# The pooling branch as fp32 matmuls over tokens, in place of GpSimd's running sums

## The chip, the cores and the metric

The kernel runs on one core of a Trainium2 chip. A core has five engines that run side by side, each from a queue of its own in order: TensorE (PE, with PEld for its weight loads), VectorE (DVE), ScalarE (ACT), GpSimd (POOL) and SyncE (SP, which issues most DMAs). They wait for each other by semaphores. The metric is the device time of one execution in microseconds (us).

## The reference, cut to what matters

Three blocks in a row over 256 tokens of width 1024, in fp32: one block of a first kind, then two layers of a second kind. Each layer of the second kind is a feed-forward, a mixer, a cross attention and a feed-forward. The mixer adds three gated branches; the change is in the pooling branch, which takes 1024 of the mixer's input columns in four groups of 256:

```python
POOL_WINDOWS = (2, 4, 8, 16)
def pool_branch(u, w_grp, scale, w_o):
    uf = u.astype(jnp.float32).reshape(B, S, POOL_GROUPS, POOL_GD)
    cz = jnp.pad(jnp.cumsum(uf, axis=1), ((0, 0), (1, 0), (0, 0), (0, 0)))
    for g, w in enumerate(POOL_WINDOWS):
        c = cz[:, :, g]
        prev = jnp.pad(c, ((0, 0), (w - 1, 0), (0, 0)))[:, :S]
        cnt = jnp.minimum(t + 1, w).astype(jnp.float32)[None, :, None]
        outs.append((c[:, 1:] - prev) / cnt)
    pooled = (jnp.stack(outs, axis=2) - uf).astype(u.dtype)
    y = jnp.einsum('bsgc,gcd->bsgd', pooled, w_grp).reshape(B, S, POOL_D) * scale
    return y @ w_o
```

So group g is the mean over the last 2, 4, 8 or 16 tokens (fewer at the start), less the token itself, and then a 256x256 product per group (`pool_w`), a scale and a 1024x1024 product (`pool_o`).

## The kernel before

Activations lie with features on the 128 partitions and the 256 tokens along the free axis. Every large product is made of *units*: 4 slices of 128 rows of the weight by 256 columns. SP loads a unit's weights (`raw_weights`, six buffers), ScalarE rounds them to a high half (L1096), DVE subtracts to get the low half (L1413; four buffers of each), three units ahead of PE. PE then runs 24 matmuls (L842, or L845 where the activations are the stationary operand and the result lies token by token, the "T form"): high by high, low by high, high by low. A `pool_w` unit has half of that, 12. One or more units that fill one of the two accumulator slots of `gemm_ps` are a *pair*; its first unit waits until the pair two before it has been copied out.

`plan` writes one list of steps, and each engine walks that list and issues its part of each step. In the mixer the list is the branch inputs, the two-map attention of eight heads spread between units, and 40 pieces of a depthwise convolution of 31 taps, each piece three taps on two features, six DVE instructions (L1854). A head is: scores on PE (L969 and L970, eight fp32 matmuls, waiting for the previous head's exponentials), row maxima on DVE (L1612), exponentials on ScalarE (L1219), normalisation on DVE, transposes on PE (the turn, L987), a copy on ScalarE (L1229), the product with the values (L1007, L1008), and the copy of the output on DVE (L1664). Every second head a norm follows (L1017 on PE, Ln and Exp with a table load each on ScalarE, L1673 on DVE).

The part that the change touches, `queries_pool`: pool group 3, group 2, query block 1, group 1, group 0, query blocks 2 and 3, two units each. DVE copies a group out of the accumulator with the token's scale (L1860), GpSimd adds shifted copies of it in `squares` (L1985, one to four doublings), multiplies by 1/count (L1990) and subtracts the input (L1993). After query block 3 ScalarE rounds the pooled tiles to `gh` (L1171, eight of them) and DVE makes `gl` (L1550, eight), and `pool_w` follows. GpSimd issues the loads of the attention bias and of the counts at the mixer's start; for the rest it only splits the feed-forward's hidden tiles.

Of the kernel before, what the change touches and what calls it, by code (L numbers as in the profile page):

```python
# [37 lines left out]
POOL_PAD = 15  # L38
# [48 lines left out]
def plan(stop=None):  # L87
# [468 lines left out]
def build(nc, a, out, scratch, marks, final, stop=None):  # L556
# [24 lines left out]
    def overlay(**shapes):  # L581

        with ExitStack() as c:
# [17 lines left out]
                  pu=[P, NF, POOL_PAD + T], tmp2=[P, NF, T], gt2=[P, 2, 2, T], bt2=[P, 2, T],  # L601
                  cnt=[P, 4, T])
# [7 lines left out]

    wide = POOL_PAD + T
    WIN = [SQ[:].rearrange("p f t -> p (f t)")[:, i * 2 * wide:(i + 1) * 2 * wide].rearrange("p (a t) -> p a t", a=2)
           for i in range(2)]
    RT8 = sb("adapt_gain", [P, NF])
    MGS = {"b1": SQ[:], "m": o_m["pu"][:, :, POOL_PAD:]}
# [47 lines left out]
    def xbuf(buf, gen):  # L663
        if buf == "G":
            return (o_b1["gh"], o_b1["gl"]) if gen in ("oa", "ob", "oc") else (o_m["gh2"], o_m["gl2"])
        if buf == "HID":
# [5 lines left out]
           "xk": o_c["xk"], "xv": o_c["xv"], "memf": o_c["memf"], "pooled": o_m["tmp2"], "TMP": o_m["tmp2"],  # L672
# [45 lines left out]
    def ready_of(k):  # L718
# [4 lines left out]
                "xq": ("o", "cross" + gen[1], f // 2), "pooled": ("pooled", gen[:2], f // 2),  # L723
# [22 lines left out]
    def _(sp):  # L746
# [29 lines left out]
        for u in raws:  # L776
# [21 lines left out]
            dst = RAWB[:, r % RAW, 0:u["nkt"], :]  # L798
# [7 lines left out]
            else:  # L806
                sp.dma_start(dst[:, :, 0:u["cols"]], w[:, :, u["col"]:u["col"] + u["cols"]]).then_inc(sems[sem], 16)
# [7 lines left out]
    def _(pe):  # L815
# [6 lines left out]
        def pe_unit(u):  # L822
# [10 lines left out]
            for c in range(tiles):  # L833
                for kt in range(u["nkt"]):
# [3 lines left out]
                    for n, (w, x) in enumerate(((WH, xh), (WH, xl), (WL, xh))):  # L838
# [5 lines left out]
                        else:  # L844
                            mm = pe.matmul(ps[:, c, 0:u["cols"]], x[:, f, c * P:(c + 1) * P],  # L845
                                           w[:, m, kt, 0:u["cols"]], start=start, stop=stop_)
            mm.then_inc(sems["gemm_done"], 1)
            up("gemm_done", ("unit", u["n"]))

# [226 lines left out]
        parts = dict(unit=pe_unit, params=pe_params, turn_x=pe_turn_x, mod=pe_mod, mod_col=pe_mod_col, bias=pe_bias, stat=pe_stat, ystat=pe_ystat,  # L1076
# [9 lines left out]
    def _(act):  # L1086
        state = dict(rq=None)
        def hi(m):
# [6 lines left out]
            s = (slice(None), m % SPLIT, slice(0, u["nkt"]), slice(0, u["cols"]))  # L1095
            act.copy(WH[s], RAWB[:, u["raw"] % RAW, 0:u["nkt"], 0:u["cols"]]).then_inc(sems["weights_rounded"], 1)  # L1096
# [278 lines left out]

        def act_evac_pool_w(k):
# [683 lines left out]
```

## Time and profile before

| | |
|---|---|
| median of 3 runs | 2508.78 us (2506.63 to 2510.61) |
| the profiled execution | 2511.45 us |
| its span, first to last instruction | 2509.6 us |
| PE busy | 2341.3 us (93%) |
| DVE busy | 1716.7 us (68%) |
| ACT busy | 1201.1 us (48%) |
| POOL busy | 136.8 us (5%) |

Busy time is a share of the whole span; what a wait costs is read in the stretch where it stands. The two mixers run from about 820 us and 1760 us; the pooling inputs stand at 919 to 1001 us and 1858 to 1942 us.

### The profile page before, as it was taken

The numbers are of one execution on the slowest core, as the hardware profiler recorded it, in microseconds if no ns is written. First come the engines' busy times: TensorE is split into PE (matmuls) and PEld (weight loads), VectorE is DVE, ScalarE is ACT, GpSimd is POOL, SyncE is SP. The second block draws the span as 40 slices with busy tenths as digits, with TensorE's granted clock in tenths as the row PEclk, the third lists the DMA queues.
The fourth block names the chain that finished last, engine by engine and source line by source line (L and its number), as shares of the span: only waits on it lengthen the run. The fifth ranks groups of instructions, "written<-read, shape, count | busy, mean of one in ns | idle before, by whom it ended". The sixth has DMA issues, their size and how long they took to land.

```text
span 2509.6 us, 43811 instructions
## 1 busy us (share of the span) xinstructions
PE 2341.3 (93%) x18041; PEld 2243.3 (89%) x18041; DVE 1716.7 (68%) x2665; ACT 1201.1 (48%) x1811; POOL 136.8 (5%) x114
## 2 busy tenths in 40 slices
PE   6998898999999988999998999999988999998997
PEld 5977898999999987889898998999987889898997
DVE  6656886886664897887555654664896877555663
ACT  2565445764444433555535444444433455535443
POOL 1000000110110012000000110110012000000110
PEclk9998999999999998999999999999997999999999
DMA  8534574667656552345444654656452336443652
GB/s 243 171 110 141 162 250 150 190 184 226 185 170 203 154 162 76 126 128 185 143 144 126 186 185 143 185 174 204 152 160 76 118 123 191 135 145 123 189 179 85
DMA packets 402038, 400.38 MB, mean 160 GB/s; under 512 B 18006, under 2 KB 399304, under 8 KB 401841
## 3 DMA queue, kind: packets, MB, share of 16 engines
q1 hardware_dynamic: 399457, 389.27, 50.3%
q0 software_dynamic: 2384, 8.32, 1.1%
q8 instruction: 144, 2.36, 0.4%
q14 instruction: 53, 0.43, 0.1%
HBM read 396.45 MB, written 1.09 MB: 158 GB/s over the span
## 4 chain that ended last, share of the span: by engine, by line
PE 71%; DVE 19%; ACT 5%; issue 4%; DMA 1%; ACTq 0%; POOL 0%; DVEq 0%; POOLq 0%
PE gemm_ps L842 59%; DVE weights_lo L1413 5%; DVE y L1854 4%; PE misc_ps L970 2%; PE misc_ps L969 2%; PE gemm_ps L845 2%; PE misc_ps L913 2%; DVE mod_partial L1510 1%; PE misc_ps L922 1%; ACT weights_hi L1096 1%; DVE y L1566 1%; ACT e L1219 1%; DVE x_res L1568 1%; ACT h_hi L1171 1%; PE misc_ps L1002 1%
## 5 line engine op out<-in xcount | busy, mean ns | idle before, releaser
L1413 DVE TENSOR_TENSOR weights_lo<-raw_weights,weights_hi 128x1024 fp32r<-128x1024 f32 x704 | 837.6, 1200 | 470.5 <-ACT weights_hi L1096 468.6
L842 PE MATMUL gemm_ps<-h_hi,weights_hi 128*128 128x256 f32 x3664 | 1054.3, 288 | 53.6 <-DVE h_lo L1547 37.3
L1096 ACT CAST weights_hi<-raw_weights 128x1024 fp32r<-128x1024 f32 x704 | 718.8, 1033 | 682.4 <-PE gemm_ps L842 623.6
L842 PE MATMUL gemm_ps<-h_lo,weights_hi 128*128 128x256 f32 x3664 | 1038.3, 283 | 0.0
L842 PE MATMUL gemm_ps<-h_hi,weights_lo 128*128 128x256 f32 x3664 | 1035.9, 283 | 0.0
L842 PEld LDWEIGHTS gemm_ps<-h_hi,weights_hi 128*128 128x128 f32 x3664 | 703.6, 192 | 64.9 <-issue 48.7
L842 PEld LDWEIGHTS gemm_ps<-h_lo,weights_hi 128*128 128x128 f32 x3664 | 703.4, 192 | 3.3 <-issue 2.2
L842 PEld LDWEIGHTS gemm_ps<-h_hi,weights_lo 128*128 128x128 f32 x3664 | 701.2, 191 | 0.0
L842 PE MATMUL gemm_ps<-hidh,weights_hi 128*128 128x256 f32 x880 | 247.8, 282 | 1.5 <-DVE weights_lo L1413 1.5
L842 PE MATMUL gemm_ps<-hidl,weights_hi 128*128 128x256 f32 x880 | 245.9, 279 | 0.0
L842 PE MATMUL gemm_ps<-hidh,weights_lo 128*128 128x256 f32 x880 | 245.7, 279 | 0.0
L1854 DVE SCALAR_TENSOR_TENSOR y<-zp,param_cols,y 128x256 f32<-128x256 f32 x480 | 213.0, 514 | 0.0
L842 PE MATMUL gemm_ps<-gh,weights_hi 128*128 128x256 f32 x544 | 163.3, 300 | 18.2 <-DVE gl L1550 14.7
L842 PEld LDWEIGHTS gemm_ps<-hidh,weights_hi 128*128 128x128 f32 x880 | 165.3, 188 | 1.9 <-DVE weights_lo L1413 1.7
L842 PEld LDWEIGHTS gemm_ps<-hidl,weights_hi 128*128 128x128 f32 x880 | 165.0, 187 | 0.2
L842 PEld LDWEIGHTS gemm_ps<-hidh,weights_lo 128*128 128x128 f32 x880 | 165.0, 188 | 0.0
L842 PE MATMUL gemm_ps<-gl,weights_hi 128*128 128x256 f32 x544 | 156.9, 288 | 0.0
L842 PE MATMUL gemm_ps<-gh,weights_lo 128*128 128x256 f32 x544 | 156.5, 288 | 0.0
L1970 POOL TENSOR_TENSOR hidl<-hf,hidh 128x512 fp32r<-128x512 f32 x55 | 73.6, 1337 | 1260.0 <-ACT hidh L1344 1260.0
L842 PEld LDWEIGHTS gemm_ps<-gh,weights_hi 128*128 128x128 f32 x544 | 107.7, 198 | 21.6 <-issue 19.2
L842 PEld LDWEIGHTS gemm_ps<-gl,weights_hi 128*128 128x128 f32 x544 | 107.8, 198 | 1.3 <-issue 1.0
L842 PEld LDWEIGHTS gemm_ps<-gh,weights_lo 128*128 128x128 f32 x544 | 107.4, 197 | 0.0
(284 smaller groups left out, 2580.6 us busy)
## 6 DMA issues: line engine op xcount, KB each, us to landing
raw_weights<-in_ffn_w_dram SPq DMA_DIRECT2D x256, 512.0 KB, 3.7
raw_weights<-in_w_in_dram SPq DMA_DIRECT2D x200, 512.0 KB, 3.6
raw_weights<-in_w_mod_dram SPq DMA_DIRECT2D x48, 512.0 KB, 5.2
raw_weights<-in_w_up_dram SPq DMA_DIRECT2D x44, 512.0 KB, 4.5
raw_weights<-in_xattn_kv_dram SPq DMA_DIRECT2D x32, 512.0 KB, 4.2
raw_weights<-in_w_out_dram SPq DMA_DIRECT2D x24, 512.0 KB, 4.5
raw_weights<-in_w_down_dram SPq DMA_DIRECT2D x20, 512.0 KB, 4.9
raw_weights<-in_w_branch_dram SPq DMA_DIRECT2D x16, 512.0 KB, 4.5
```

Of the source, the lines that this page charges most:

```text
L842: mm = pe.matmul(ps[:, c, 0:T], w[:, m, kt, c * P:(c + 1) * P], x[:, f, :], start=start, stop=stop_)
L845: mm = pe.matmul(ps[:, c, 0:u["cols"]], x[:, f, c * P:(c + 1) * P], w[:, m, kt, 0:u["cols"]], start=start, stop=stop_)
L913: mm = pe.matmul(STAT[:, 0:T], ONES[:], squares[:, f, :], start=f == 0, stop=f == NF - 1)
L922: mm = pe.matmul(STAT[:, 0:T], ONES[:], SQ[:, f, :], start=f == 0, stop=f == NF - 1)
L969: pe.matmul(ps, c["q"][m][:, qt * P:(qt + 1) * P], c["k"][m][:, 0:nk], start=True, stop=False)
L970: mm = pe.matmul(ps, FLIP[:], c["hank"][:, c["head"][m], T - nk:T], start=False, stop=True)
L1002: mm = pe.matmul(PV[:, f * T:(f + 1) * T], c["v"][f][kb], PT[:, kb * T:(kb + 1) * T], start=kb == 0, stop=kb == 1)
L1096: act.copy(WH[s], RAWB[:, u["raw"] % RAW, 0:u["nkt"], 0:u["cols"]]).then_inc(sems["weights_rounded"], 1)
L1171: act.activation(h[:, k["ft0"] + f, :], src, ACT.Copy, scale=col(c[0], c[1] + f) if c else scale).then_inc(sems["act_split"], 1)
L1413: dve.tensor_tensor(WL[s], RAWB[:, u["raw"] % RAW, 0:u["nkt"], 0:u["cols"]], WH[s], ALU.subtract).then_inc(sems["weights_rest"], 1)
L1854: dve.scalar_tensor_tensor(out=Y[:, f, :], in0=o_m["zp"][:, f, j:j + T], scalar=col(f"dw{l}", 8 * j + f), in1=Y[:, f, :], op0=ALU.mult, op ...
L1970: pool.tensor_tensor(l_[:, s, :], src, h[:, s, :], ALU.subtract).then_inc(sems["hidden_rest"], 1)
```

## The change

The constant 256x256 matrix of a group holds 1/count where the token is within the window, less the identity. Pooling is then a product over tokens, for which the input must lie with tokens on the partitions. So the pool inputs are computed in the T form, in two pairs of 512 columns (groups 2 and 3, then 0 and 1), each of four units of 2 slices by 512 columns, 12 matmuls each. DVE copies such a pair out with two instructions. A new step `window` per group runs four fp32 matmuls on PE: the matrix is lower triangular in tokens, so the second half of the tokens needs only 128 result columns. Its result takes an accumulator slot. ScalarE rounds it from there to `gh` and DVE subtracts to `gl`; the eight splits are gone, and so are GpSimd's sums. The load of the counts becomes one of the matrices, 128x1536 numbers instead of 128x1024.

```diff
         def queries_pool():
-            for name, j in (("pool", 3), ("pool", 2), ("q", 1), ("pool", 1), ("pool", 0), ("q", 2), ("q", 3)):
-                if name == "q":
-                    z2(l, "q", j, "evac_scaled", dst="q", ft=2 * j, by=HD ** -0.5)
-                else:
-                    z2(l, "pool", j, "evac_pool", ft=2 * j)
-                    add("window", g=j, l=l)
-            for g in (3, 2, 1, 0):
-                for f in (2 * g, 2 * g + 1):
-                    add("split", buf="G", gen=key + "p", src="pooled", f=f, ft0=0, after=readers.get("G"), v=0)
+            after = readers.get("G")
+            def inputs(j):
+                z2(l, "pool", j, "evac_v2", form="T", cols=2 * COLS, dst="pt", c0=j * COLS)
...
+            def window(g):
+                p = dict(id=len(pairs), l=l, g=g, gen=key + "p", after=after)
+                pairs.append(p)
+                add("window", **p)
+                add("evac_window", **p)
+            inputs(2)
+            query(1)
+            window(3)
+            inputs(0)
+            window(2)
+            query(2)
+            window(1)
+            query(3)
+            window(0)
...
+        def pe_window(k):
+            ps, u, g = GP[:, k["id"] % 2, :, :], BUF["pt"], k["g"]
+            pe.wait_ge(*done(("evac", k["id"] - 2)))
+            pe.wait_ge(*done(("tm", "pt", k["l"], g * COLS)))
+            pe.wait_ge(sems["windows_in"], at("win", k["l"]))
+            for i in range(2):
+                f = 2 * g + i
+                pe.matmul(ps[:, i, 0:T], u[:, 0, f * P:(f + 1) * P], o_m["win"][:, g, 0:T], start=True, stop=False)
+                mm = pe.matmul(ps[:, i, P:T], u[:, 1, f * P:(f + 1) * P], o_m["win"][:, g, T:T + P], start=False, stop=True)
...
+        def act_window(k):
+            f = 2 * k["g"]
+            act.wait_ge(sems["gemm_done"], at("pooled", k["l"], k["g"]))
...
+            act.copy(o_m["gh2"][:, f:f + 2, :], slot(k["id"])).then_inc(sems["act_split"], 1)
...
+        def vec_window(k):
+            f = 2 * k["g"]
+            dve.wait_ge(sems["act_split"], at("split_hi", "G", k["gen"], f))
+            dve.tensor_tensor(o_m["gl2"][:, f:f + 2, :], slot(k["id"]), o_m["gh2"][:, f:f + 2, :], ALU.subtract).then_inc(sems["vec_split"], 1)
...
+            mark(("evac", k["id"]), "vec_split")
```

Where it moves instructions. On PE in layer 0, behind query block 1 and the value product of head 0, before (L842: a unit; `vec_conv` is the copy-out of pool group 2, long before):

```order
L1007 MATMUL misc_ps<-pt,v 128x256 [waits act_attn]
L1008 MATMUL misc_ps<-pt,v 128x128
L842 MATMUL gemm_ps<-h_hi,weights_hi 128x256 [waits vec_split,vec_conv,weights_rest]
L842 MATMUL gemm_ps<-h_lo,weights_hi 128x256
L842 MATMUL gemm_ps<-h_hi,weights_lo 128x256
```

The same place of the change (L876, L877: the window; `pu` holds the inputs token by token; L863: a wide unit; its `vec_drain` is now the copy-out of query block 1):

```order
L1038 MATMUL misc_ps<-pt,v 128x256 [waits act_attn]
L1039 MATMUL misc_ps<-pt,v 128x128
L876 MATMUL gemm_ps<-win,pu 128x256 [waits windows_in,vec_drain]
L877 MATMUL gemm_ps<-win,pu 128x128
L876 MATMUL gemm_ps<-win,pu 128x256
L877 MATMUL gemm_ps<-win,pu 128x128
L863 MATMUL gemm_ps<-weights_hi,h_hi 128x512 [waits vec_split,vec_drain,weights_rest]
```

The four matmuls of group 3 have moved in as a pair of their own, and the pair behind them waits for another copy-out than before.

On DVE, from the softmax of head 1 to the convolution piece behind, before:

```order
L1648 SCALAR_TENSOR_TENSOR e<-e,rden 128x256
L1664 COPY q<-misc_ps 128x256
L1594 SCALAR_TENSOR_TENSOR q<-gemm_ps,rstd_x 128x512
L1413 TENSOR_TENSOR weights_lo<-raw_weights,weights_hi 128x1024 x2
L1854 SCALAR_TENSOR_TENSOR y<-zp,param_cols,y 128x256 x6
L1860 TENSOR_TENSOR pu<-gemm_ps,rstd_x 128x2x256
```

and of the change:

```order
L1687 SCALAR_TENSOR_TENSOR e<-e,rden 128x256
L1703 COPY q<-misc_ps 128x256
L1632 SCALAR_TENSOR_TENSOR q<-gemm_ps,rstd_x 128x512
L1898 TENSOR_TENSOR gl<-gemm_ps,gh 128x512
L1451 TENSOR_TENSOR weights_lo<-raw_weights,weights_hi 128x1024 x2
L1891 SCALAR_TENSOR_TENSOR y<-zp,param_cols,y 128x256 x6
```

The copy-out of query block 1 (L1594, now L1632) stands where it stood, behind the softmax; the subtraction of window 3 follows it, and the copy-out of a pool group behind the convolution piece is gone.

On PE in front of `pool_w`, the change has window 0 between the value product of head 2 and the first `pool_w` matmul:

```order
L1039 MATMUL misc_ps<-pt,v 128x128
L876 MATMUL gemm_ps<-win,pu 128x256 [waits windows_in,vec_drain,vec_split]
L877 MATMUL gemm_ps<-win,pu 128x128
L876 MATMUL gemm_ps<-win,pu 128x256
L877 MATMUL gemm_ps<-win,pu 128x128
L860 MATMUL gemm_ps<-gh,weights_hi 128x256 [waits vec_split,vec_drain,weights_rest]
```

Before, `pool_w` stood right behind the value product. Its `vec_drain` is the copy-out of query block 3, its `vec_split` the pooled low half.

## Rows read from the trace of the kernel before

**Rows 1.** The page's chain of work that ended last, by engine.

```profile
PE 71%; DVE 19%; ACT 5%; issue 4%; DMA 1%; ACTq 0%; POOL 0%; DVEq 0%; POOLq 0%
```

**Rows 2.** PE's waits, 905 to 1060 us: total, times, longest in us.

```profile
PE gemm_ps L842 <- DVE gl L1550: 7.4, 1, 7.4
PE misc_ps L969 <- ACT e L1219: 6.8, 2, 6.1
```

**Rows 3.** The same view, 1845 to 2000 us.

```profile
PE misc_ps L969 <- ACT e L1219: 7.6, 2, 6.7
PE gemm_ps L842 <- DVE gl L1550: 7.3, 1, 7.3
```

**Rows 4.** DVE's timeline, layer 0: start us, duration us, instruction.

```profile
927.75 0.69 DVE L1860 TENSOR_TENSOR pu<-gemm_ps,rstd_x 128x512 f32<-128x512 f32 x1
...
929.49 7.90 DVE L1854 SCALAR_TENSOR_TENSOR y<-zp,param_cols,y 128x256 f32<-128x256 f32 x6
937.31 1.01 DVE L1612 TENSOR_REDUCE neg_max<-misc_ps 128x2 f32<-128x256 f32 x2
...
942.85 2.46 DVE L1854 SCALAR_TENSOR_TENSOR y<-zp,param_cols,y 128x256 f32<-128x256 f32 x6
```

**Rows 5.** GpSimd's timeline, the sums of group 3.

```profile
928.53 2.00 POOL L1985 TENSOR_TENSOR squares<-pu 128x540 f32<-128x540 f32 x1 [118.54 <-DVE pu L1860]
...
935.87 1.24 POOL L1993 TENSOR_TENSOR tmp<-tmp,pu 128x512 f32<-128x512 f32 x1
```

**Rows 6.** PE's timeline: scores (L969), turns (L987), the norm's sum (L1017), `pool_w` (gh).

```profile
924.33 0.48 PE L969 MATMUL misc_ps<-k,q 64*128 64x128 f32 x2
...
940.13 0.79 PE L969 MATMUL misc_ps<-k,q 64*128 64x128 f32 x2 [6.11 <-ACT e L1219]
...
951.59 0.49 PE L987 MATMUL misc_ps<-ident,e 128*128 128x128 f32 x3
...
962.66 0.46 PE L969 MATMUL misc_ps<-k,q 64*128 64x128 f32 x2 [1.45 <-DVE q L1594]
...
982.22 0.49 PE L969 MATMUL misc_ps<-k,q 64*128 64x128 f32 x2
...
989.13 0.49 PE L987 MATMUL misc_ps<-ident,e 128*128 128x128 f32 x3
989.46 1.02 PE L1017 MATMUL misc_ps<-small_squares,ones 128*128 128x512 f32 x2
...
1001.28 0.55 PE L842 MATMUL gemm_ps<-gh,weights_hi 128*128 128x256 f32 x1 [7.42 <-DVE gl L1550]
...
1863.42 0.48 PE L969 MATMUL misc_ps<-k,q 64*128 64x128 f32 x2
...
1941.97 0.55 PE L842 MATMUL gemm_ps<-gh,weights_hi 128*128 128x256 f32 x1 [7.32 <-DVE gl L1550]
```

**Rows 7.** The chain that ended last, in order of time: start us, us, what.

```profile
952.08 2.83 PE gemm_ps L842 x24
954.91 0.43 PE misc_ps L1007 x2
955.34 0.22 PE misc_ps L1008 x2
...
961.92 0.61 DVE q L1594
```

**Rows 8.** Stretches: length, busy us of PE, PEld, DVE, ACT, POOL, PEclk, DMA share, GB/s.

```profile
940.10:951.60 11.50, 11.47 (x41) 8.44 (x42) 6.86 (x15) 1.86 (x2) 5.24 (x5) 0.56 0.30 93
1001.20:1005.90 4.70, 4.62 (x24) 4.52 (x24) 4.70 (x13) 1.86 (x4) 0.00 (x0) 0.61 0.14 24
1020.40:1030.50 10.10, 10.04 (x62) 8.03 (x63) 9.98 (x22) 6.38 (x11) 0.00 (x0) 1.00 0.34 104
1941.90:1947.30 5.40, 5.33 (x25) 5.23 (x25) 5.40 (x15) 1.94 (x4) 0.00 (x0) 0.53 0.27 72
1961.70:1971.80 10.10, 10.07 (x41) 7.78 (x42) 10.02 (x22) 3.81 (x6) 0.00 (x0) 0.66 0.33 105
```

More of the change, by code:

```diff
@@ L37 @@
 FFN_K = 3
-POOL_PAD = 15
 LAYERS = 2
@@ L609, in build @@
     o_b1["bt1"] = o_b1["rg"][:, 0]
-    wide = POOL_PAD + T
-    WIN = [SQ[:].rearrange("p f t -> p (f t)")[:, i * 2 * wide:(i + 1) * 2 * wide].rearrange("p (a t) -> p a t", a=2)
-           for i in range(2)]
     RT8 = sb("adapt_gain", [P, NF])
-    MGS = {"b1": SQ[:], "m": o_m["pu"][:, :, POOL_PAD:]}
+    MGS = {"b1": SQ[:], "m": o_m["pu"][:]}
     last_x = max([k["v"] for kind, k in steps if kind == "residual"], default=0)
@@ L683, in slot, with unit_of @@
         return GP[:, pid % 2, :, 0:T]
+    def unit_of(buf, i, u):
+        if u["cols"] <= COLS:
+            return buf[:, i, 0:u["nkt"], 0:u["cols"]]
+        wide = buf[:, i].rearrange("p k n -> p (k n)").rearrange("p (k n) -> p k n", n=u["cols"])
+        return wide[:, 0:u["nkt"], :]
     def att(cfg, i):
@@ L1074, in pe_finish @@
             up("pe_setup", ("out_ps",))
-        parts = dict(unit=pe_unit, params=pe_params, turn_x=pe_turn_x, mod=pe_mod, mod_col=pe_mod_col, bias=pe_bias, stat=pe_stat, ystat=pe_ystat,
+        parts = dict(unit=pe_unit, window=pe_window, params=pe_params, turn_x=pe_turn_x, mod=pe_mod, mod_col=pe_mod_col, bias=pe_bias, stat=pe_stat, ystat=pe_ystat,
                      rstd_cols=pe_rstd_cols, qk_norm=pe_qk_norm, scores=pe_scores, turn=pe_turn, pv=pe_pv,
@@ L1374, in act_cln_out @@
             up("act_conv", ("cln_tanh", l, p))
+        def act_window(k):
+            f = 2 * k["g"]
+            act.wait_ge(sems["gemm_done"], at("pooled", k["l"], k["g"]))
+            if k["after"] is not None:
+                act.wait_ge(sems["gemm_done"], at("unit", k["after"]))
+            act.copy(o_m["gh2"][:, f:f + 2, :], slot(k["id"])).then_inc(sems["act_split"], 1)
+            up("act_split", ("split_hi", "G", k["gen"], f))
         def act_evac_pool_w(k):
@@ L1600, in vec_v2 @@
             for t in range(TT):
-                dve.tensor_scalar(BUF[k["dst"]][:, t, k["c0"]:k["c0"] + COLS], slot(k["id"])[:, t, :], RT[:, t:t + 1], None, ALU.mult).then_inc(sems["vec_drain"], 1)
+                dve.tensor_scalar(BUF[k["dst"]][:, t, k["c0"]:k["c0"] + k["cols"]], GP[:, k["id"] % 2, t, 0:k["cols"]], RT[:, t:t + 1], None, ALU.mult).then_inc(sems["vec_drain"], 1)
                 up("vec_drain", ("evac", k["id"]))
             mark(("tm", k["dst"], k["l"]), "vec_drain")
-            mark(("tm", k["dst"], k["l"], k["c0"]), "vec_drain")
+            for c in range(k["c0"], k["c0"] + k["cols"], COLS):
+                mark(("tm", k["dst"], k["l"], c), "vec_drain")
         def vec_softmax(k):
@@ L1856, in vec_conv31 @@
             mark(("conv", l), "vec_conv")
[L1858 to L1862 removed]
+        def vec_window(k):
+            f = 2 * k["g"]
+            dve.wait_ge(sems["act_split"], at("split_hi", "G", k["gen"], f))
+            dve.tensor_tensor(o_m["gl2"][:, f:f + 2, :], slot(k["id"]), o_m["gh2"][:, f:f + 2, :], ALU.subtract).then_inc(sems["vec_split"], 1)
+            up("vec_split", ("split", "G", k["gen"], f))
+            mark(("split", "G", k["gen"], f + 1), "vec_split")
+            mark(("evac", k["id"]), "vec_split")
         def vec_pool_w(k):
@@ L1949, in pool_hankel @@
             if k["which"] == 2:
-                pool.dma_start(o_m["cnt"][:], bass.AP(tensor=a["inv_count"].tensor, offset=0, ap=[[0, P], [1, 4 * T]])).then_inc(sems["count_in"], 16)
-                up("count_in", ("cnt", k["l"]), by=16)
+                pool.dma_start(o_m["win"][:], a["windows"]).then_inc(sems["windows_in"], 16)
+                up("windows_in", ("win", k["l"]), by=16)
         def pool_blocks(k):
@@ L2033, in shape_constants @@
     t = np.arange(T)
-    inv = np.stack([(1.0 / np.minimum(t + 1, w)).astype(np.float32) for w in (2, 4, 8, 16)])
+    windows = []
+    for w in (2, 4, 8, 16):
+        behind = t[None, :] - t[:, None]
+        share = (1.0 / np.minimum(t + 1, w)).astype(np.float32)
+        m = np.where((behind >= 0) & (behind < w), share[None, :], np.float32(0.0)) - np.eye(T, dtype=np.float32)
+        windows.append(np.concatenate([m[:P], m[P:, P:]], axis=1))
+    windows = np.ascontiguousarray(np.stack(windows, axis=1).astype(np.float32))
     return {"ident": np.eye(P, dtype=np.float32), "flip": np.ascontiguousarray(np.eye(P, dtype=np.float32)[::-1]),
-            "headsum": heads, "onehot": np.ascontiguousarray(onehot), "inv_count": inv}
+            "headsum": heads, "onehot": np.ascontiguousarray(onehot), "windows": windows}
 def declare(nc, arrays):
```

70 lines of the change are left out of this document (23 added, 47 removed).

## The prediction

> **What bounds the kernel now.** The first view is the page's chain that ended last: 71% of it is TensorE (PE), 19% VectorE (DVE), and nothing to speak of is GpSimd (POOL) [rows 1]. So GpSimd's sums are worth nothing by themselves; they count where they hold up DVE, and through it PE. The next view is PE's waits inside the two mixers, where the change lies. Layer 0: 7.4 us once for the low half `gl` of the pooled input, and 6.8 us for ScalarE's exponentials `e`, of which 6.1 in one wait [rows 2]; layer 1: 7.3 and 7.6, of which 6.7 in one [rows 3]. The third view says why the exponentials are late. DVE's queue is in order: copy-out of pool group 3 at 927.75, a weight subtraction, six convolution taps, then the row maxima that ScalarE's exponentials wait for. Those six taps took 7.90 us; the same six took 2.46 us at 942.85 [rows 4]. In just that time GpSimd ran the sums of group 3, from 928.53 to 937.11 [rows 5]. So 5.44 us of the first wait are GpSimd's doing.
>
> The Trainium skill says that GpSimd shares its SBUF interfaces with VectorE and contends with DVE instructions that have two SBUF inputs ("GPSIMD Engine Reference", section 8, Key points). The taps read two, and [rows 4, 5] agree with it in direction; by that page alone the change could only be a gain.
>
> **The yardstick.** I measure from the first score matmul of head 0 (call it A: 924.33 and 1863.42) to the first `pool_w` matmul (1001.28 and 1941.97) [rows 6]. That is 76.95 us in layer 0 and 78.55 us in layer 1. I build the same stretch for the changed kernel out of pieces of this trace.
>
> **Prices.** A unit of 24 matmuls of 256 columns is 2.83 us, 0.118 us each [rows 7]. A wide unit is 12 of 512 columns, which no row shows. Upper bound: twice 0.118, so 2.83 us again. Lower bound: the fp32 rows take 0.22 us for 128 columns and 0.43 for 256 [rows 7], time in proportion to columns with the weight load hidden; at half of 0.43 for 512 columns of this type, 12 x 0.215 = 2.6 us. I take 2.7. A window group is two matmuls of 256 and two of 128 columns in fp32; the attention value product is one of each, with the same operand shapes, at 0.43 + 0.22 = 0.65 us [rows 7], so 1.3 us a group. If they went like the scores, whose eight matmuls (four of 256 columns, four of 128) are 6.91 - 2.83, some 3.9 to 4.1 us (982.22 to 989.13, less a unit) [rows 6, 7], four would be 2.0 us; the shapes speak for 1.3. The four groups are 5.2 us a layer of new PE work. A DVE read of 512 columns from PSUM is 0.61 us in the chain [rows 7].
>
> **What the change puts in the way.** The accumulator has two slots, and a pair (a set of units that fills one slot) waits until the pair two before it is copied out. Before, the pair between was always two units, 5.65 us of cover. Now each window is a pair of its own, of only 1.3 us. So the unit behind window 3 waits for the copy-out of query block 1, the unit behind window 2 for that of the pool inputs 0 and 1, and `pool_w` behind window 0 for that of query block 3. All three copy-outs stand on DVE behind a whole softmax and behind the copy of the previous head's output. Behind the wait PE's entire queue stands, and through freed weight buffers ScalarE's roundings and SP's loads.
>
> **The stretch, step by step.**
> 1. Head 0. Row maxima began at A+12.98 [rows 4]. Take off 5.44 (no GpSimd) and 0.6 (no copy-out of group 3): A+6.94. Scores of head 1 began 2.82 later (937.31 to 940.13) [rows 4, 6]: A+9.76. PE arrives at 3.9 + 2 x 2.7 = 9.3, so a wait of about 0.4 is left of 6.1.
> 2. Scores and one unit, to the turn (transposes) of head 0: 6.91 (982.22 to 989.13) [rows 6]. From a turn through ScalarE's copy, a weight rounding, the subtraction, six taps, softmax, output copy and the copy-out of the query block until PE goes on: 11.07 (951.59 to 962.66) [rows 6]. The unit behind window 3 starts at A+27.74. PE's own work since the turn (0.3 + 2.83 + 0.65 + 1.3) is 5.1, so it waits 6.0 us.
> 3. Two wide units 5.4, scores and a wide unit 6.8, the same relay 11.07, and 0.6 because the wide copy-out takes two instructions: A+51.6. PE waits here about 6.7.
> 4. Two units 5.65, scores, unit and turn 7.24 (982.22 to 989.46) [rows 6], window 1 in front of them 1.3: the sub-norm matmul at A+65.8. From there to `pool_w` it was 11.82 (989.46 to 1001.28) [rows 6]: the norm's Ln and Exp on ScalarE, softmax, copy, copy-out of query block 3, and the first split of the pooled input. Only that split, 0.35, leaves: A+77.2. PE waits 5.8 instead of 7.4. The splits were the name on that wait, not its reason.
>
> **The clock.** After such a wait PE runs at the lower of its two levels (1.2 of 2.4 GHz) for a while. In the stretch behind the 7.42 wait the granted clock was 0.61, so 0.39 x 4.70 = 1.8 us were lost; behind the 7.32 wait 0.47 x 5.40 = 2.5; behind the 6.11 wait, with scores first, 0.44 x 11.5 = 5.1 [rows 8]. Behind the two new waits dense units come first, so I take 2.2 for each, 4.4 a layer. The third has the cost it had.
>
> The skill's "TensorE: Matmul & The Clock Gate" (section "A second HAM failure mode") speaks against this change: cycling through PSUM between groups of matmuls makes PE idle often enough that the clock swings. By that rule the waits cost more than 2.2 each; the third rival has this.
>
> Layer 0: 77.2 + 4.4 - 76.95 = +4.7. Layer 1: 77.2 + 4.4 - 78.55 = +3.1. Then three small terms. Behind `pool_w` DVE now has one subtraction (0.6) where eight splits stood (2.8), so the later short waits for exponentials go (6.8 less 6.1 is 0.7; 7.6 less 6.7 is 0.9) [rows 2, 3]: -1.6. The 0.9 one was followed by a clock of 0.66 over 10.10 us, 3.4 us lost; the 0.7 one by none [rows 8]: -3.4. The new wait of 0.4 before scores may do the same in either layer; one in four each: +1.7. Sum: +4.7 + 3.1 - 1.6 - 3.4 + 1.7 = **+4.5 us**.
>
> What is hidden costs nothing. GpSimd's queue gets emptier; the window load (0.8 MB instead of 0.5) is issued over 100 us before its use (GpSimd then waited 118.54 us for the first copy-out) [rows 5]. ScalarE's four copies replace eight of half their size. DVE stands for window 1 until PE has done it, with a weight subtraction and six taps behind, but the norm on ScalarE ends later than they do. If that cover were gone, it would cost the 3 us of these.
>
> The profiled execution took 2511.45 us (span 2509.6), 2.7 more than the median of 2508.78; the sum is a difference and goes on the median: 2513.3 us.
>
> **Rivals.**
> - *The waits stay, the clock doesn't fall.* The windows put work into stretches that were idle. Then the four losses of 2.2 go: 4.5 - 8.8 = -4.3, 2504.5 us. Against it: all three waits over 6 us in [rows 8] had a drop behind them.
> - *Not slower: the slot waits are covered.* If DVE reached the three copy-outs a softmax earlier, PE would be limited by its own work: 76.95, less waits of 15.0 (7.4, 6.1 and the 1.45 at 962.66), less the clock losses of 5.1 and 1.8, plus 5.2, less 1.1 for eight wide units, is 59.2, so 18 less a layer, some 2473 us. It is decided at the first unit behind window 3: a wait under 1 us there says this case. For it: DVE loses 0.6 us of copy-out and GpSimd's brake, and so starts earlier. Against: the relay of 11.07 us ran without GpSimd beside it at the end, its length is set by the queue's order, and it starts with PE's own turn, so an earlier DVE doesn't shorten it.
> - *Each new wait costs as much clock as the 6.11 one did.* 5.1 instead of 2.2 four times is +11.6, and 3.4 for the short wait where it comes in both layers: 2525 to 2530 us.
> - *The fp32 windows are dearer.* Only window 1 is on the path; at 2.0 us instead of 1.3 it is +1.4 in all: inside the range.
>
> **How the numbers follow.** Forecast 0.6, with its own range: clock 1.8 to 2.5 a wait (-1.6, +1.2), the short-wait clock none or both (-1.7, +5.1), the 3.4 of layer 1 stays (+3.4), wide units and windows (-0.6, +2), so 2509 to 2522 where not all come together. Clock-free rival 0.17, covered waits 0.1, dear clock 0.13. What a measurement tells from no change is 0.2%, 5 us. Faster takes the covered waits and a part of the clock-free case: 0.14. Slower takes half of the forecast's chance, which straddles +5, and the dear case: 0.43. The rest is within: 0.43. The range 2504 to 2526 leaves out the covered waits and half of the dear clock.
>
> **What would show it.** The 6.1 and 6.7 us waits for `e` gone; six taps at 2.46 us behind head 0's scores; three PE waits a layer of about 6, 6.7 and 5.8 us whose releasers are the copy-outs of `q`, the pool inputs and `q`; granted clock down behind each; windows 1.3 us a group. Wrong would be a first unit behind window 3 that starts at once, or a granted clock of 1 behind the waits.

## The result and the profile after

| | median | range, runs |
|---|---|---|
| before | 2507.09 us | 2503.07 to 2510.61, 6 |
| changed | 2522.89 us | 2513.12 to 2527.81, 6 |

The ratio is 1.0056, 95% interval 1.0043 to 1.0068: slower by 14 us by this ratio (the two medians are 15.8 apart), where +4.5 was forecast. Direction and range (2504 to 2526) held, the size did not. The profiled execution took 2524.09 us, its span is 2522.3; before it was 2509.6, so the two traces have +12.7 us between them to explain.

The chain that ended last looks as it did in [rows 1], with one point less of DVE, and one more each of PE and of waiting for nothing shown:

```profile
PE 72%; DVE 18%; ACT 5%; issue 5%; DMA 1%; POOL 0%; ACTq 0%; DVEq 0%; POOLq 0%
```

PE's waits, 905 to 1060 us (total, times, longest in us), which answer to [rows 2]; layer 1 reads the same within 0.1 us:

```profile
PE gemm_ps L860 <- issue: 12.2, 2, 6.5
PE gemm_ps L863 <- issue: 6.0, 2, 5.8
PE misc_ps L1000 <- ACT e L1249: 1.1, 2, 0.7
```

Where one wait of 7.4 us and one of 6.1 stood, there are three of about 6. They carry no releaser ("issue"), so the view doesn't say what they are for; the order does (the slot's copy-out), and PE's and DVE's timelines, laid beside each other, confirm it. In a timeline row the square brackets hold the idle time in front of the instruction and what ended it. PE in layer 0, answering to [rows 6] (L1000 scores, L1018 turn, L876 window, L863 first wide unit behind window 3, L860 the unit behind window 2 and `pool_w`):

```profile
922.39 0.48 PE L1000 MATMUL misc_ps<-k,q 64*128 64x128 f32 x2
...
932.64 0.49 PE L1000 MATMUL misc_ps<-k,q 64*128 64x128 f32 x2 [0.42 <-ACT e L1249]
...
943.26 0.60 PE L876 MATMUL gemm_ps<-win,pu 128*128 128x256 f32 x2
...
950.58 0.77 PE L863 MATMUL gemm_ps<-weights_hi,h_hi 128*128 128x512 f32 x1 [5.84 <-issue]
...
977.63 0.55 PE L860 MATMUL gemm_ps<-h_hi,weights_hi 128*128 128x256 f32 x1 [6.48 <-issue]
...
1006.20 0.55 PE L860 MATMUL gemm_ps<-gh,weights_hi 128*128 128x256 f32 x1 [5.74 <-issue]
...
1025.90 0.48 PE L1000 MATMUL misc_ps<-k,q 64*128 64x128 f32 x2 [0.70 <-ACT e L1249]
```

DVE behind the scores of head 0, answering to [rows 4], and the three copy-outs that the long waits end on (the first with the output copy in front of it):

```profile
927.44 2.46 DVE L1891 SCALAR_TENSOR_TENSOR y<-zp,param_cols,y 128x256 f32<-128x256 f32 x6
929.82 1.01 DVE L1651 TENSOR_REDUCE neg_max<-misc_ps 128x2 f32<-128x256 f32 x2
...
949.46 0.42 DVE L1703 COPY q<-misc_ps 128x256 f32<-128x256 f32 x1
949.79 0.68 DVE L1632 SCALAR_TENSOR_TENSOR q<-gemm_ps,rstd_x 128x512 f32<-128x512 f32 x1
...
976.13 1.40 DVE L1639 TENSOR_SCALAR pu<-gemm_ps,rstd_tok 128x512 f32<-128x512 f32 x2
...
1005.42 0.68 DVE L1632 SCALAR_TENSOR_TENSOR q<-gemm_ps,rstd_x 128x512 f32<-128x512 f32 x1
```

The six taps take 2.46 us instead of 7.90, and the wait for `e` in front of head 1's scores is 0.42 instead of 6.11. PE goes on at 950.58, 0.1 us behind the end (950.47) of the copy-out of query block 1. PE had been idle since the end of window 3, 5.84 us. The other two agree: the copy-out of the pool inputs 0 and 1 ends at 977.53 and PE goes on at 977.63, that of query block 3 ends at 1006.10 and PE goes on at 1006.20.

The stretches behind the waits, answering to [rows 8] (length, busy us of PE, PEld, DVE, ACT, POOL, granted clock, DMA share, GB/s):

```profile
950.50:959.10 8.60, 8.52 (x25) 6.57 (x25) 3.31 (x5) 1.05 (x1) 0.00 (x0) 0.65 0.13 31
977.60:986.30 8.70, 8.67 (x49) 8.57 (x49) 4.72 (x9) 0.62 (x1) 0.00 (x0) 0.65 0.27 81
1006.20:1011.50 5.30, 5.30 (x25) 5.16 (x26) 4.90 (x11) 1.78 (x4) 0.00 (x0) 0.54 0.34 102
1025.90:1036.00 10.10, 10.10 (x41) 7.80 (x42) 10.03 (x22) 3.77 (x6) 0.00 (x0) 0.66 0.35 105
1975.10:1985.20 10.10, 10.10 (x42) 7.56 (x43) 10.03 (x22) 3.72 (x6) 0.00 (x0) 0.66 0.34 105
```

Lost clock is one less the granted share, times the length: 3.0, 3.0, 2.4 and 3.4 us in layer 0. The work behind each wait runs part of its time at 1.2 instead of 2.4 GHz.

The kernel before had two such losses that [rows 8] leave out, behind the waits of 1.45 and 1.76 us of head 2's scores for the copy-out of query block 1:

```profile
962.60:972.70 10.10, 10.04 (x41) 7.35 (x42) 6.29 (x10) 0.36 (x1) 4.57 (x4) 0.66 0.30 80
1901.80:1913.30 11.50, 11.41 (x40) 8.61 (x41) 6.32 (x10) 0.39 (x1) 5.49 (x4) 0.55 0.23 68
```

They are 3.4 and 5.2 us. The forecast isn't touched, since it took the scores from a row without such a loss, but the covered-waits rival is, and so is the last experiment.

| from head 0's first scores (A) to `pool_w` | before | forecast | after |
|---|---|---|---|
| layer 0 | 76.95 | 81.6 | 83.81 |
| layer 1 | 78.55 | 81.6 | 83.03 |

So 6.9 and 4.5 of the 12.7 us lie in the two stretches. From layer 0's `pool_w` to layer 1's A it is another 4.1 us (862.14 before, 866.21 after), of which the clock behind the short wait at 1025.90 is 3.4 and that behind `pool_w` 0.6. From layer 1's `pool_w` to the end it is -0.8, and the start of the kernel gave 1.9 us back before the change is reached (A at 922.39 instead of 924.33).

### The profile page after: what moved, and what is told of

Read it like the earlier page. It is cut to its first block, busy times and chain, and to the rows that moved or that the text cites. A ratio compares the mean times of both kernels' runs of the same rounds, so it can differ in the third digit from the quotient of the medians.

```text
span 2522.3 us, 43491 instructions
## 1 busy us (share of the span) xinstructions
PE 2346.2 (93%) x17913; PEld 2239.0 (89%) x17913; DVE 1700.7 (67%) x2655; ACT 1200.3 (48%) x1803; POOL 87.9 (3%) x78
## 4 chain that ended last, share of the span: by engine, by line
PE 72%; DVE 18%; ACT 5%; issue 5%; DMA 1%; POOL 0%; ACTq 0%; DVEq 0%; POOLq 0%
PE gemm_ps L860 58%; DVE weights_lo L1451 5%; DVE y L1891 4%; PE gemm_ps L863 3%; PE misc_ps L1001 2%; PE misc_ps L1000 2%; PE misc_ps L944 2%; PE misc_ps L953 1%; DVE mod_partial L1548 1%; ACT weights_hi L1126 1%; DVE y L1604 1%; DVE x_res L1606 1%; ACT e L1249 1%; ACT h_hi L1201 1%; PE misc_ps L1033 1%
## 5 line engine op out<-in xcount | busy, mean ns | idle before, releaser
L860 PE MATMUL gemm_ps<-h_hi,weights_hi 128*128 128x256 f32 x3536 | 1017.5, 288 | 66.4 <-DVE h_lo L1585 37.2
L860 PE MATMUL gemm_ps<-h_lo,weights_hi 128*128 128x256 f32 x3536 | 1002.4, 283 | 0.0
L860 PE MATMUL gemm_ps<-h_hi,weights_lo 128*128 128x256 f32 x3536 | 1000.0, 283 | 0.0
L860 PEld LDWEIGHTS gemm_ps<-h_hi,weights_hi 128*128 128x128 f32 x3536 | 679.1, 192 | 77.7 <-issue 62.4
L860 PEld LDWEIGHTS gemm_ps<-h_lo,weights_hi 128*128 128x128 f32 x3536 | 679.0, 192 | 3.4 <-issue 2.7
L860 PEld LDWEIGHTS gemm_ps<-h_hi,weights_lo 128*128 128x128 f32 x3536 | 677.1, 191 | 0.0
L860 PE MATMUL gemm_ps<-hidh,weights_hi 128*128 128x256 f32 x880 | 247.6, 281 | 1.5 <-DVE weights_lo L1451 1.5
L860 PE MATMUL gemm_ps<-hidl,weights_hi 128*128 128x256 f32 x880 | 245.7, 279 | 0.0
L860 PE MATMUL gemm_ps<-hidh,weights_lo 128*128 128x256 f32 x880 | 245.4, 279 | 0.0
L1891 DVE SCALAR_TENSOR_TENSOR y<-zp,param_cols,y 128x256 f32<-128x256 f32 x480 | 196.6, 477 | 0.0
L860 PE MATMUL gemm_ps<-gh,weights_hi 128*128 128x256 f32 x544 | 163.6, 301 | 14.5 <-issue 12.0
L860 PEld LDWEIGHTS gemm_ps<-hidh,weights_hi 128*128 128x128 f32 x880 | 165.3, 188 | 1.9 <-DVE weights_lo L1451 1.7
L860 PEld LDWEIGHTS gemm_ps<-hidl,weights_hi 128*128 128x128 f32 x880 | 164.9, 187 | 0.2
L860 PEld LDWEIGHTS gemm_ps<-hidh,weights_lo 128*128 128x128 f32 x880 | 165.1, 188 | 0.0
L860 PE MATMUL gemm_ps<-gl,weights_hi 128*128 128x256 f32 x544 | 157.1, 289 | 0.0
L860 PE MATMUL gemm_ps<-gh,weights_lo 128*128 128x256 f32 x544 | 156.7, 288 | 0.0
L860 PEld LDWEIGHTS gemm_ps<-gh,weights_hi 128*128 128x128 f32 x544 | 108.1, 199 | 17.9 <-issue 15.7
L860 PEld LDWEIGHTS gemm_ps<-gl,weights_hi 128*128 128x128 f32 x544 | 108.0, 199 | 1.4 <-issue 1.0
L860 PEld LDWEIGHTS gemm_ps<-gh,weights_lo 128*128 128x128 f32 x544 | 107.6, 198 | 0.0
```

The lines of the kernel that those rows point to most:

```text
L860: mm = pe.matmul(ps[:, c, 0:T], w[:, m, kt, c * P:(c + 1) * P], x[:, f, :], start=start, stop=stop_)
L1891: dve.scalar_tensor_tensor(out=Y[:, f, :], in0=o_m["zp"][:, f, j:j + T], scalar=col(f"dw{l}", 8 * j + f), in1=Y[:, f, :], op0=ALU.mult, op ...
```

## The experiments

**Theory:** the fp32 work costs nothing by itself. What costs is that a window takes an accumulator slot of its own, so that the pair behind it waits for a copy-out that stands on DVE behind a softmax; and each such wait is paid again in clock. **Rivals:** the PE time of the fp32 and wide matmuls; and the relay through turn, ScalarE and value product, which would set the pace whatever the order of the copy-outs. In all ratios of this section "before" is the kernel before on the same chip: 2506.72 us for the first four, 2507.21 for the next three, 2508.16 for the last.

### Windows without slots of their own

```diff
             def window(g):
-                p = dict(id=len(pairs), l=l, g=g, gen=key + "p", after=after)
-                pairs.append(p)
+                return dict(l=l, g=g, gen=key + "p", after=after)
...
-            ps, u, g = GP[:, k["id"] % 2, :, :], BUF["pt"], k["g"]
+            ps, u, g = GP[:, k["id"] % 2, :, T:], BUF["pt"], k["g"]
```

with the order inputs 2 and 3, query 1 and window 3, inputs 0 and 1, query 2 and window 2, query 3 and window 1, `pool_w` of group 3 and window 0. Where query block and window share a bank, the copy-outs of both stand behind both, in order. (The Trainium skill asks for that: "PSUM — Partial Sum Buffer", section "PSUM bank collisions raise a hardware error", has it that two engines may not be in one bank of one quadrant of 32 partitions together, whatever the columns. No run here shows it.)

> The changed kernel, except that a window is no pair of its own: its result goes into the unused columns 256 to 511 of the accumulator slot of the pair next to it (window 3 with query block 1, 2 with 2, 1 with 3, 0 with the first pool_w product), and window 2 stands behind query block 2. All arithmetic stays. Theory (the slot waits and the clock losses behind them are what makes the changed kernel slower): the three PE waits of 5.7 to 6.5 us a layer shrink to under 1.5 us each, the stretch from the first scores to pool_w falls from 83.8 and 83.0 us to 60 to 70 us, and the whole to 2470 to 2500 us. Rival (the 5.2 us of fp32 matmuls a layer and the wide units are the cost): the stretch stays over 78 us, the whole over 2512 us.

Measured: 2487.38 us, ratio 0.9918 (0.9904 to 0.9932). The stretch is 61.82 us in layer 0 and 58.61 in layer 1; the first `pool_w` product starts without a wait. The theory holds and the rival falls: the same matmuls are all there. One wait is left, the second `pool_w` product, and what stands before it on DVE is again a softmax, an output copy and the copy-out of query block 3 (PE's timeline, DVE's, and the stretch behind, apart):

```profile
991.78 0.55 PE L865 MATMUL gemm_ps<-gh,weights_hi 128*128 128x256 f32 x1 [3.66 <-DVE gl L1906]
```

```profile
989.91 0.42 DVE L1711 COPY q<-misc_ps 128x256 f32<-128x256 f32 x1
990.25 0.68 DVE L1640 SCALAR_TENSOR_TENSOR q<-gemm_ps,rstd_x 128x512 f32<-128x512 f32 x1
990.85 0.68 DVE L1906 TENSOR_TENSOR gl<-gemm_ps,gh 128x512 fp32r<-128x512 f32 x1
```

```profile
991.70:1001.70 10.00, 9.92 (x29) 6.78 (x29) 8.98 (x20) 3.44 (x6) 0.00 (x0) 0.50 0.34 107
```

This wait of 3.66 us took another 5.0 us of clock; behind it stood scores. The 3.2 us between the two layers' stretches are clock, too: in layer 0 it fell behind the wait of 0.41 us of head 1's scores (0.66 over the 10.1 us from 933.5), in layer 1 behind the same wait it stayed at 1.00.

### Useless work in the waits

```diff
-            for i in range(2):
+            for i in [i for _ in range((5, 1, 5, 5)[g]) for i in range(2)]:
                 f = 2 * g + i
                 pe.matmul(ps[:, i, 0:T], u[:, 0, f * P:(f + 1) * P], o_m["win"][:, g, 0:T], start=True, stop=False)
```

> The changed kernel with the four matmuls of windows 3, 2 and 0 run five times over (the same result written again), 5.2 us of additional TensorE work in front of each of the three long waits of 5.84, 6.48 and 5.74 us; window 1 once. Theory (the additional work is hidden in the wait, and a TensorE that isn't idle keeps its clock): the six waits fall to about 1 us, the granted clock behind them is 1 instead of about 0.6, each saves 2.6 us, in all -15 us: about 2507 us, although 31 us of work was added. Rival (the clock falls anyway, or the waits only cost their length): within 3 us of the changed kernel, 2520 to 2526 us. Second rival (TensorE is the bound there): +31 us, 2553 us.

Measured: 2506.64 us, ratio 0.9991 (0.9979 to 1.0003), as expected to 1 us: 31 us of TensorE work added, 16 us gained on the changed kernel. PE's waits, 905 to 1060 us, and the stretches behind the three:

```profile
PE gemm_ps L860 <- issue: 1.7, 2, 1.2
PE gemm_ps L863 <- issue: 0.7, 2, 0.5
```

```profile
951.20:957.10 5.90, 5.83 (x25) 4.48 (x25) 3.27 (x4) 2.18 (x3) 0.00 (x0) 1.00 0.18 46
975.60:981.50 5.90, 5.85 (x49) 5.74 (x49) 4.66 (x9) 1.00 (x2) 0.00 (x0) 1.00 0.31 91
1001.40:1004.50 3.10, 3.03 (x25) 2.93 (x25) 2.87 (x7) 2.06 (x5) 0.00 (x0) 1.00 0.16 25
```

The same 25 to 49 instructions that took 8.6, 8.7 and 5.3 us now take 5.9, 5.9 and 3.1: 2.7, 2.8 and 2.2 us less, and in layer 1 2.2, 2.5 and 2.0: 14.4 us in all. The relay is as it was (turn to unit 11.02 us, 940.24 to 951.26). So the price of the six drops is measured, 14 to 16 us, as much as the change lost in all. It doesn't follow that the drops are the whole difference: the kernel before has drops of its own, and the changed kernel keeps its waits.

The Trainium skill warns of this ("TensorE: Matmul & The Clock Gate", section "A second HAM failure mode"): in a bf16 kernel, PE idling between groups of matmuls while it cycles through PSUM made its clock swing. This trace agrees in direction, and has the price: 2.0 to 2.8 us for a wait, on top of its length.

### Every window twice

```diff
-            for i in range(2):
+            for i in [i for _ in range(2) for i in range(2)]:
```

> The changed kernel with the four matmuls of every window run twice (the same result written again): +1.3 us of TensorE work per window, 10.4 us in all. Theory (windows 3, 2 and 0 stand in front of waits and are hidden, only window 1 lies on the path): +1.3 us a layer, 2.6 us in all, the three waits 1.3 us shorter each: 2524 to 2527 us. Rival (the fp32 matmuls' own time is what the change costs): +10.4 us, 2533 us.

Measured: 2517.93 us, ratio 1.0045 (1.003 to 1.006), which is not told from the changed kernel's 1.0056 (1.0043 to 1.0068). The rival's 2533 us is excluded: the PE time of the windows is hidden, but for window 1. In the trace the stretch grew by 1.27 us in layer 0 (85.08), as worked out from window 1, by 0.50 in layer 1 (83.53), and each wait lost what the window gained:

```profile
950.33 0.77 PE L863 MATMUL gemm_ps<-weights_hi,h_hi 128*128 128x512 f32 x1 [4.44 <-issue]
...
977.37 0.55 PE L860 MATMUL gemm_ps<-h_hi,weights_hi 128*128 128x256 f32 x1 [5.18 <-issue]
...
1007.23 0.44 PE L860 MATMUL gemm_ps<-gh,weights_hi 128*128 128x256 f32 x1 [4.33 <-issue]
```

That the whole came out below the expectation, not above the changed kernel, fits the clock behind the short waits for `e` of head 5's scores: in this trace none of the two had a drop behind it, in the changed kernel's both had one (last two rows of the stretches above), 3.4 us each. One trace of each kernel can't say more.

### The kernel before without GpSimd's sums

```diff
-            for lev in range(g + 1):
...
-            pool.tensor_tensor(p, p, u[:, :, POOL_PAD:], ALU.subtract).then_inc(sems["pool_window"], 1)
...
+            mark(("pooled", f"l{k['l']}", k["ft"] // 2), "vec_conv")
```

> The kernel before without GpSimd's work: the shifted additions, the multiplication by 1/count and the subtraction are left out, and the splits read the pool inputs themselves, so the pooling isn't computed. Theory (GpSimd beside DVE stretched the six convolution taps by 5.4 us, and this was the reason of the 6.1 and 6.7 us waits for the exponentials and of the clock loss behind them): both waits under 1 us, the wait in front of pool_w stays at 7, the first-scores-to-pool_w stretch 5 to 10 us shorter in each layer: 2488 to 2498 us. Rival (the wait is given back later by the relay behind the turn): within 4 us of the kernel before, 2503 to 2510 us.

Measured: 2489.03 us, ratio 0.9924 (0.9907 to 0.9942). The six taps, and PE's waits, 905 to 1060 us:

```profile
928.05 2.46 DVE L1854 SCALAR_TENSOR_TENSOR y<-zp,param_cols,y 128x256 f32<-128x256 f32 x6
```

```profile
PE gemm_ps L842 <- DVE gl L1550: 7.3, 1, 7.3
...
PE misc_ps L969 <- ACT e L1219: 1.4, 2, 0.9
```

The long wait for `e` is gone, the one in front of `pool_w` is not, and the stretches are 66.90 and 63.85 us, 10.1 and 14.7 shorter, where 5 to 10 were expected. The surplus in layer 1 is clock: behind the wait of 1.76 us of head 2's scores, where the kernel before lost 5.2 us, it stayed at 1.00 (in layer 0 it fell as before, 0.66 over 10.1 us). Taking GpSimd away was worth 18 us: the change had this gain in hand, and its slot waits used it up.

### Copy-outs ahead of the softmax, slots as in the change

A copy-out marked `early` is issued right behind the last unit of its pair, ahead of the softmax that stood between. On PE nothing moves but window 0, which now stands ahead of the value product of head 2.

```diff
-            query(1)
+            query(1, early=True)
             window(3)
-            inputs(0)
+            inputs(0, early=True)
             window(2)
             query(2)
             window(1)
-            query(3)
-            window(0)
+            query(3, early=True)
+            window(0, early=True)
```

> The changed kernel with its windows as pairs of their own, but on DVE and ScalarE the copy-outs of query block 1, of the pool inputs 0 and 1, and of query block 3 with window 0 stand ahead of the softmax that stood in front of them. Nothing else is moved, all slots are as in the changed kernel. Theory (a slot that is freed late is the cause, and late means behind the softmax): the three waits of 5.8, 6.5 and 5.7 us fall under 1.5 us each, the stretch from the first scores to pool_w falls from 83 to 60 to 66 us, the whole to 2475 to 2492 us. Rival (the turn, ScalarE's copy and the product with the values set the pace, whatever the order of the copies): the waits stay over 4 us, the whole over 2512 us.

Measured: 2478.70 us (2477.14 to 2481.84, 4 runs), ratio 0.9894 (0.9879 to 0.991): 1.1% ahead of the kernel before. The stretch is 62.05 us in layer 0 and 61.95 in layer 1 (1847.27 to 1909.22). The copy-out of query block 1 is at A+20.50 (A is 921.78 here), 6.9 us earlier than the A+27.40 of the changed kernel, and the output copy of the softmax behind it comes 0.8 us later, at A+27.88 instead of A+27.07 (DVE):

```profile
942.28 0.69 DVE L1637 SCALAR_TENSOR_TENSOR q<-gemm_ps,rstd_x 128x512 f32<-128x512 f32 x1
942.89 2.46 DVE L1896 SCALAR_TENSOR_TENSOR y<-zp,param_cols,y 128x256 f32<-128x256 f32 x6
...
949.66 0.42 DVE L1708 COPY q<-misc_ps 128x256 f32<-128x256 f32 x1
```

and PE in front of and behind the first `pool_w` product:

```profile
983.83 0.36 PE L865 MATMUL gemm_ps<-gh,weights_hi 128*128 128x256 f32 x1 [1.00 <-DVE weights_lo L1456]
...
992.92 0.35 PE L865 MATMUL gemm_ps<-gh,weights_hi 128*128 128x256 f32 x1 [1.62 <-issue]
997.22 0.36 PE L865 MATMUL gemm_ps<-gh,weights_hi 128*128 128x256 f32 x1 [0.98 <-issue]
```

So it is not that windows have slots, but that the slots in front of them are freed late. The second rival falls: the relay sets the pace only because the copy-outs were put behind it.

### Both remedies

The kernel without slots for windows, with one copy-out moved as well:

```diff
-            query(3, 1)
+            query(3, 1, early=True)
```

> The kernel of half_slots_b, with one thing moved: on DVE and ScalarE the copy-outs of query block 3 and of window 1 (which shares its slot) stand ahead of the softmax of head 3 instead of behind it. Theory (what is left there is the same kind of wait: in half_slots_b the second pool_w product waited 3.66 and 3.77 us for the copy-out of query block 3 behind a softmax, and the clock fell behind it to half for some 10 us): this wait under 0.5 us, the clock kept, 2 x (3.7 + 3 to 5) us less than 2487: 2470 to 2477 us, faster than both kernels. Rival (the softmax starts later by the copy-outs, so the wait comes back at the next scores): 2483 to 2490 us.

Measured: 2480.08 us (2478.20 to 2482.33, 4 runs), ratio 0.9896 (0.9883 to 0.991): a gain of 7 us on the kernel without slots, not the 10 to 17 expected nor the rival's 4 at most, and the same as the kernel above within the measurement. The wait for query block 3 is gone, but another took most of its place, for the copy-out of the first `pool_w` product, which shares its slot with window 0 and so stands behind it and behind six taps:

```profile
994.55 0.36 PE L867 MATMUL gemm_ps<-gh,weights_hi 128*128 128x256 f32 x1 [2.98 <-DVE gl L1919]
```

The granted clock behind it is 0.66 over 10.0 us, another 3.4 us.

### The same remedy without the change

First only the splits, moved ahead of query block 3 in the kernel before:

```diff
+                if (name, j) == ("q", 3):
+                    for g in (3, 2, 1, 0):
+                        for f in (2 * g, 2 * g + 1):
+                            add("split", buf="G", gen=key + "p", src="pooled", f=f, ft0=0, after=after, v=0)
```

> The kernel before, GpSimd's sums and all, with the eight splits of the pooled input moved ahead of query block 3, where the sums have long been done. Theory (the 7.4 us wait in front of pool_w has the copy-out of query block 3 behind the softmax as its reason, not the splits): the first pool_w product starts at once, but the second waits some 5 to 6 us for the slot of query block 3; 0 to 3 us a layer are gained: 2500 to 2507 us. Rival (the splits are the reason): both start without a wait over 1 us, 2 x (7.4 + 2) us are gained, 2488 us.

Measured: 2515.62 us, ratio 1.0038 (1.0026 to 1.0051): slower, which neither side expected. The first `pool_w` product starts at once (994.47, A+69.33), the second waits (layer 0):

```profile
1004.13 0.55 PE L844 MATMUL gemm_ps<-gh,weights_hi 128*128 128x256 f32 x1 [8.05 <-issue]
```

The splits were the name on the 7.4 us wait; with them gone from there, the copy-out of query block 3 alone makes PE wait: that part of the theory holds. The size doesn't: the wait is 8.05, not 5 to 6. Head 4's scores come at A+81.81, where they came at A+81.57, so nothing was gained, and they now run behind a fresh wait at half clock (0.50 over the 6.0 us from 1004.0): the next turn is at A+91.39 instead of A+87.07, 4.3 us, and in layer 1 3.3 us later than before (A+92.56, was A+89.25).

Then the splits and the copy-out of query block 3, both ahead of the softmax:

```diff
-                    z2(l, "q", j, "evac_scaled", dst="q", ft=2 * j, by=HD ** -0.5)
+                    z2(l, "q", j, "evac_scaled", dst="q", ft=2 * j, by=HD ** -0.5, early=j == 3)
...
-                    add("split", buf="G", gen=key + "p", src="pooled", f=f, ft0=0, after=readers.get("G"), v=0)
+                    add("split", buf="G", gen=key + "p", src="pooled", f=f, ft0=0, after=readers.get("G"), v=0, early=True)
```

> The kernel before, GpSimd's sums and all, with the copy-out of query block 3 and then the eight splits moved ahead of the softmax of head 3: the same remedy as in own_early, without the change to TensorE. Theory (in front of pool_w the kernel before had the same disease as the changed kernel, and GpSimd's brake on the taps is the other half): the 7.4 and 7.3 us waits fall under 2 us, the 6.1 and 6.7 us waits for the exponentials stay; 5 to 8 us a layer are gained, 2490 to 2498 us, and own_early at 2478.7 stays 11 us or more ahead. Rival (the order alone makes own_early fast, and TensorE's pooling adds nothing): 2475 to 2482 us.

Measured: 2503.05 us (12 runs), ratio 0.9986 (0.9975 to 0.9997). This order alone gives 5 us of the 28 that the four copy-outs give together with the change. The theory overrated it, too:

```profile
996.74 0.35 PE L847 MATMUL gemm_ps<-gh,weights_hi 128*128 128x256 f32 x1 [2.59 <-DVE gl L1555]
1001.68 0.68 PE L974 MATMUL misc_ps<-k,q 64*128 64x128 f32 x2 [1.88 <-ACT e L1224]
```

Eight splits, 2.8 us in all, in front of the softmax make head 3's exponentials late (1.88 us), and the clock falls behind that wait instead of the other (0.55 over 9.0 us from 1001.0). Head 4's scores come at A+77.26, 4.3 us earlier than before, but the turn behind them at A+87.07, exactly where it was: in layer 0 the fall of the clock takes the whole lead. In layer 1, where that wait is 0.53 us and the clock behind it stays at 1.00, the turn is 3.8 us earlier (A+85.41, was A+89.25).

The rival isn't excluded in full. In `own_early` the copy-out of query block 1 went ahead of a softmax, too; here it stayed, and its waits are still in this trace (1.44 and 1.76 us in front of head 2's scores). In the kernel before these waits and the clock behind them were 1.45 + 3.4 and 1.76 + 5.2 us. So an estimate from these rows is that the order alone could give up to 12 us more, 17 of the 28. No run tried it.

## Why the prediction was right in direction and short in size

- **The brake.** Right: six taps 2.46 us, the wait for `e` 0.42 us (0.4 forecast). Scores of head 1 at A+10.25, forecast A+9.76. The half microsecond is DVE's, which has no gap here: the copy-out of query block 0 begins 1.33 us ahead of A (921.06), where it was 1.82 ahead (922.51), so the row maxima begin at A+7.43 instead of A+6.94. The wide unit was too cheap as well, but that was hidden, since PE waited for `e` all the same. It was taken at 2.7 us, and two of them took 5.94 (926.28 to 932.22). Twelve matmuls of 512 columns follow each other at 0.234 us, 2.8 in all, twice the 0.118 of 256 columns. The upper bound (2.83) was the right end, and the shape that I took the lower one from, fp32, is no guide.
- **The relay and the three waits.** Right, nearly to the tenth. From turn to the unit behind window 3 it was 11.03 us (forecast 11.07). The waits are 5.84, 6.48 and 5.74 (forecast 6.0, 6.7, 5.8). Window 3 takes 1.3 us. The rival of covered waits was refuted at the point it named, the first unit behind window 3. It came true only once the waits for slots were gone. That its 59.2 us for the stretch was close to the 58.6 to 62.1 then measured is partly luck: it left the clock loss behind the 1.45 us wait in the stretch (3.4 us), without which its sum is 55.8. Its 2473 us was not reached: 2478.7.
- **The clock behind the new waits: mis-sized.** 2.2 us each was taken, 3.0 measured in layer 0 (3.0, 3.0), 2.4 and 2.8 in layer 1; +0.8 each in layer 0. I had averaged two rows of [rows 8], both of `pool_w`, whose units are short; the third one, 5.1 us, is scores behind a wait. Behind the new waits stand one or two units and then scores, between the two. The dear-clock rival (5.1) overshot by 2.1 to 2.7 a wait; that its 2525 us lies nearer to the measured time than 2513.3 is luck, but for its term of 3.4 us behind the short wait in both layers, which came true. `pool_w` itself lost 2.4 instead of 1.8.
- **The short waits: wrong.** The forecast had them go (-1.6), and layer 1's clock loss with them (-3.4), because DVE has one subtraction where eight splits stood. Both are there: 0.70 in each layer, and the clock fell behind both, in layer 0 too, where it hadn't before (3.4 more). The step that failed took the splits to be in this wait's path. They aren't: from head 4's scores to head 5's it is 14.57 us before (1005.90 to 1020.47) and 14.51 after (1011.39 to 1025.90). The chain in between starts on PE: scores, a unit and the turn (1016.84), then ScalarE's copy of the turn and of a `pool_w` product and its rounding of a weight (to 1019.5), then DVE's weight subtraction, six taps and row maxima (from 1023.07), then the exponentials. DVE stands idle in it (1.86 us in front of a subtraction at 1018.32, before 0.21), so with fewer splits it only waits longer.
- **The risk taken for the 0.4 us wait** (+1.7) did not come: the granted clock behind it is 1.00 in both layers. It did come behind 0.41 us in layer 0 of both kernels without slots for windows (0.66 over 10 us), so the risk was real.

Added up: the two stretches 2.2 and 1.4 over the forecast (in layer 0 0.5 of it by the row maxima, 1.6 by the clock), short waits 1.6, their clock 3.4 and 3.4, less 1.7, is +10.3; less 1.9 at the kernel's start gives 8.4. The miss between the spans is 12.7 - 4.5 = 8.2. The median's miss (2522.89 against 2513.3, 9.6) is 1.4 more, which is within the spread of the runs.

What stays open: what makes the clock fall behind a short wait. In the kernel with filled waits it fell behind 0.57 us in layer 0 (0.66 over 10.1 us) and stayed at 1.00 behind 0.79 us in layer 1, with the same instructions. No run tried to steer it.

## What to carry to other kernels

A new step that borrows a buffer between two others costs what its neighbours then wait for, not what it runs: ask of each wait it creates what stands in front of the releasing instruction on its in-order engine, and move that instruction ahead before moving work. Here the change alone lost 14 us and the change with four copy-outs issued earlier gained 28, of which up to 17 might have been had by the order alone (an estimate, untested). Charge a wait of TensorE twice, once for its length and once for the clock behind it, and count that second part by what runs there.

## What the hardware showed unexpectedly

- Idle TensorE time is dearer than busy time: 31 us of repeated matmuls in the waits made the kernel 16 us faster (2522.89 to 2506.64). The granted clock behind the waits went from 0.54 to 0.70 to 1.00 in all six.
- Behind a wait of 3.66 us the loss was 5.0 us (0.50 over 10.0) with scores there, behind 6.48 us it was 3.0 with two dense units there. In these rows what runs next says more than how long the wait was.
- Short waits for `e` of 0.41 to 0.91 us had a clock drop of 3.4 us behind them in some layers of some kernels and none in others. Even 1.76 us of waiting for `q` had a loss of 5.2 us behind it in one kernel and none in another. The changed kernel's runs spread over 14.7 us (2513.12 to 2527.81), those before over 7.5; whether that is the same toss was not settled.
- GpSimd's sums stretched six DVE instructions with two SBUF inputs from 2.46 to 7.90 us; taking them out of an otherwise unchanged kernel gave 18 us, though GpSimd is no part of the chain that ended last.
